# Input projection of a hybrid attention and Fourier layer: products of 2304 tokens, or seven block products in three passes

## The reference

```python
h = _rmsnorm(x, norm_g) * (1 + scale) + shift      # scale, shift, gate from silu(cond) @ w_ada + b_ada
z = h @ w_in                                       # 1024 -> 6176 channels
q, k, v, gate_a, r_f, r_b, u, gate_b, mg_a, mg_b = jnp.split(z, idx, axis=-1)
q, k = rope(q), rope(k); q = q * HEAD_DK ** -0.5
g_f = log_sigmoid(r_f @ w_af + b_af) / 16          # g_b likewise, from r_b
o = gla_scan(q, k, v, g_f) + reversed gla_scan(..., g_b)
y_a = (_rmsnorm(o) * silu(gate_a)) @ w_proj_a
y_b = (real(fft2(u)) @ w_four * silu(gate_b)) @ w_proj_b
x = x + gate * ((sigmoid(mg_a) * y_a + sigmoid(mg_b) * y_b) @ w_out)
```

## Time and profile before

| | |
|---|---|
| Runs | 2262.85, 2268.07, 2270.06 us; median 2268.07 |
| Profiled execution, from the first to the last instruction (span) | 2259.7 us |
| The shown median beside this span | 8.4 us above it |
| Instructions | 33049, of these 12121 matmuls |
| PE, PEld, DVE, ACT, POOL busy | 94%, 82%, 32%, 27%, 20% |
| DMA | 340.70 MB, 151 GB/s on average |

### The profile page before, as it was taken

The page is one execution under the profiler, slowest core; times in us unless marked ns, Lnnn a source line. Parts: engine busy times, 40 slices in busy tenths (PEclk is TensorE's granted clock), DMA queues, the critical chain, the costliest instruction groups (busy, mean ns, idle before and its releaser), DMA issues.

```text
span 2259.7 us, 33049 instructions
## 1 busy us (share of the span) xinstructions
PE 2129.4 (94%) x12121; PEld 1845.1 (82%) x12121; DVE 721.1 (32%) x1255; ACT 613.5 (27%) x1384; POOL 451.4 (20%) x340
## 2 busy tenths in 40 slices
PE   7699999999999999999999989998957999998998
PEld 2488889999888888888888867776857999997886
DVE  2867771000010001001001005557687222223423
ACT  2646661111111111111111116766523011012221
POOL 1500000000433223142322310004242111111212
PEclk9899999999999999999999989999978999999999
DMA  7334442212545445454544557554133343454443
GB/s 299 115 109 155 152 158 75 83 61 83 176 150 186 150 159 174 159 173 154 182 153 155 170 171 312 215 205 165 47 149 124 113 125 116 121 189 153 132 147 112
DMA packets 178437, 340.70 MB, mean 151 GB/s; under 512 B 14610, under 2 KB 120268, under 8 KB 173360
## 3 DMA queue, kind: packets, MB, share of 16 engines
q1 hardware_dynamic: 178352, 339.64, 43.2%
HBM read 215.84 MB, written 123.74 MB: 150 GB/s over the span
## 4 chain that ended last, share of the span: by engine, by line
PE 79%; issue 7%; DVE 6%; DMA 3%; ACT 3%; POOL 1%; SPq 0%; POOLq 0%; ACTq 0%; DVEq 0%
PE bank L1409 44%; PE bank L1613 15%; PE bank L1470 9%; PE bank L1498 3%; PE bank L1517 1%; PE bank L1519 1%; PE bank L1518 1%; PE bank L1505 1%; DMA x_in<-in_x 1%; ACT junk L770 1%; DVE zb L384 1%; POOL yt L750 1%; DVE uf L1267 1%; DVE h L1023 1%; PE bank L1526 1%
## 5 line engine op out<-in xcount | busy, mean ns | idle before, releaser
L1409 PE MATMUL bank<-h_hi,w_hi 128*128 128x512 f32 (+1 forms) x1640 | 606.3, 370 | 6.7 <-POOL h_lo L691 5.6
L1409 PE MATMUL bank<-h_lo,w_hi 128*128 128x512 f32 (+1 forms) x1640 | 605.4, 369 | 0.0
L1409 PE MATMUL bank<-h_hi,w_lo 128*128 128x512 f32 (+1 forms) x1640 | 604.4, 369 | 0.0
L1409 PEld LDWEIGHTS bank<-h_hi,w_hi 128*128 128x128 f32 x1640 | 310.2, 189 | 59.6 <-issue 5.8
L1409 PEld LDWEIGHTS bank<-h_hi,w_lo 128*128 128x128 f32 x1640 | 309.9, 189 | 52.5
L1409 PEld LDWEIGHTS bank<-h_lo,w_hi 128*128 128x128 f32 x1640 | 310.3, 189 | 51.5
L1057 DVE CAST w_hi<-w_raw 128x1024 fp32r<-128x1024 f32 x48 | 36.6, 762 | 870.2 <-PE bank L1409 672.8
L845 ACT ACTIVATE stage<-bank 128x512 f32<-128x512 f32 (+1 forms) x160 | 88.7, 555 | 682.0 <-PE bank L1409 682.0
L1613 PE MATMUL bank<-in_hi,pw_hi 128*128 128x256 f32 x864 | 245.9, 285 | 12.2 <-DVE in_lo L1292 12.2
L1613 PE MATMUL bank<-in_lo,pw_hi 128*128 128x256 f32 x864 | 245.6, 284 | 0.0
L1613 PE MATMUL bank<-in_hi,pw_lo 128*128 128x256 f32 x864 | 245.6, 284 | 0.0
(11 more groups left out here) (178 smaller groups left out, 2876.1 us busy)
## 6 DMA issues: line engine op xcount, KB each, us to landing
w_raw<-in_w_in SPq DMA_DIRECT2D x49, 512.0 KB, 3.9
dec_in<-e_dram SPq DMA_DIRECT2D x48, 384.0 KB, 3.5
rope<-in_rope SPq DMA_DIRECT2D x48, 384.0 KB, 4.1
qk_dec<-dec_in SPq DMA_DIRECT2D x48, 384.0 KB, 2.9
mg_ld<-mg_dram SPq DMA_DIRECT2D x72, 256.0 KB, 2.9
e_dram<-decs SPq DMA_DIRECT2D x32, 512.0 KB, 3.0
mg_dram<-stage SPq DMA_DIRECT2D x64, 256.0 KB, 2.0
wada<-in_w_ada SPq DMA_DIRECT2D x6, 2048.0 KB, 8.1
```

The costliest lines, as they stand in the source:

```text
L1409: ins = pe.matmul(bank[out][:, 0:n], w[0][:, k, sl], h[:, k, t0:t0 + n], start=(k == 0 and w is w_hi and h is h_hi), stop=(k == KT - 1 and ...
```

## The change

The input projection is written anew; the rank unit, the decays and the rotations are part of it.

- Tokens are taken in 3 passes of 768. In a pass, h is cut into four blocks: two halves of the inner dimension (A11 and A12, A21 and A22: 512 each) by two blocks of 384 tokens. The weights of a pair of units (2 x 128 channels) are cut the same way. Seven products of such blocks or of sums of them, 12 matmuls of 384 columns each (`product`), give the four quarters of the result, instead of eight. One pair of units is a window; a pass has 24 (`PAIRS`).
- POOL makes the sums of h once a pass (`sum_inputs`, `last_sum`) and the sums of weights for each window (`sum_weights`, 4 of 512 elements). ACT makes the high part of each of the seven weight operands of the next window (`high_weights`), DVE the low part (`low_weights`).
- The quarters are put together from PSUM in two banks and three tiles: ACT copies product 0 (`copy_first`) and moves out the first quarter (`first_quarter`), DVE makes five sums (`add_product`). Product 2 waits for the copy, product 3 for the first sum, 5 for the second and 6 for the third.
- Eight windows of a pass (`GATE_WINDOWS`) also make the gates of a head: two logit matmuls, two rounds of Relu, Abs, Exp, Ln on ACT, scans and a difference on DVE (`gate_sums`), two Exps on ACT (`decays`).
- q and k stay on chip: SP swaps their halves by a DMA within SBUF, POOL rotates (`rotate`, 3 instructions of 768 elements) and multiplies by the decays (`decay`, 1536 elements), and only qk_dec is stored. q_dram and e_dram go.
- v is made with channels in partitions and turned by PE transposes in the next window. The x tiles of the next pass are normalised, turned and modulated in windows 13 to 18, and split in window 23. Two adaLN rows move to the last pass.

The diff, cut to its core:

```diff
-RB = 384
+NP = 3
+BW = 384
+PW = 2 * BW
+TP = PW // P
+HK = KT // 2
+PAIRS = ([("qk", 0), ("u", 0), ("v", 0), ("qk", 1), ("u", 1), ("v", 1), ("qk", 2), ("v", 2), ("qk", 3), ("v", 3)]
+         + [("ga", i) for i in range(4)] + [("gb", i) for i in range(2)] + [("mg", i) for i in range(8)])
+NW = len(PAIRS)
+NPROD = 7
+RING = 8
+GATE_WINDOWS = (1, 2, 4, 5, 7, 8, 10, 11)
+X_WINDOWS = tuple(range(13, 13 + TP))
+ADA_WINDOWS = (15, 16)
+LOW_POOL_H = (4, 6)
...
-            def unit_block(slot, b, a, out):
-                t0, n = BLOCKS[b]
-                sl = slice(P * slot, P * slot + P)
-                for k in range(KT):
-                    for w, h in ((w_hi, h_hi), (w_hi, h_lo), (w_lo, h_hi)):
-                        ins = pe.matmul(bank[out][:, 0:n], w[0][:, k, sl], h[:, k, t0:t0 + n],
-                                        start=(k == 0 and w is w_hi and h is h_hi), stop=(k == KT - 1 and w is w_lo))
-                ins.then_inc(s_mm, 1)
...
+            def product(p, w, j):
+                n = NW * p + w
+                m = NPROD * n + j
+                slot = m % RING
+                bnk = bank[3 * (n % 2) + (0, 1, 0, 1, 2, 1, 2)[j]]
+                pe.wait_ge(s_wlo, m + 1)
+                if w == 0:
+                    input_split(p, j)
+                if j == 0 and n >= 2:
+                    pe.wait_ge(s_c11, n - 1)
+                elif j == 1 and n >= 2:
+                    pe.wait_ge(s_d, 5 * (n - 2) + 4)
+                elif j == 2:
+                    pe.wait_ge(s_p1, n + 1)
+                elif j == 3:
+                    pe.wait_ge(s_d, 5 * n + 1)
+                elif j == 4 and n >= 2:
+                    pe.wait_ge(s_d, 5 * (n - 2) + 5)
+                elif j == 5:
+                    pe.wait_ge(s_d, 5 * n + 2)
+                elif j == 6:
+                    pe.wait_ge(s_d, 5 * n + 3)
+                first = j in (0, 1, 4)
+                for k in range(HK):
+                    for wt, h in ((w_hi, h_hi), (w_hi, h_lo), (w_lo, h_hi)):
+                        ins = pe.matmul(bnk[:, 0:BW], wt[slot][:, k, :], h[:, j, k, :],
+                                        start=(first and k == 0 and wt is w_hi and h is h_hi),
+                                        stop=(k == HK - 1 and wt is w_lo),
+                                        skip_group_check=not first)
+                ins.then_inc(s_p, 1)
...
+            for p in range(NP):
+                for w in range(NW):
+                    uses = window_uses(p, w)
+                    for j in range(NPROD):
+                        product(p, w, j)
+                        for u in uses[j]:
+                            use(p, w, u)
...
+            def low_weights(n, j):
+                if n > LAST:
+                    return
+                m = NPROD * n + j
+                dve.wait_ge(s_whi, m + 1)
+                dve.tensor_tensor(w_lo[m % RING][:, :, :], w_op(n, j), w_hi[m % RING][:, :, :].bitcast(F32), ALU.subtract
+                                  ).then_inc(s_wlo, 1)
...
+            def add_product(n, step):
+                p, w, kind, i = pair(n)
+                b_bank, e_bank = bank[3 * (n % 2) + 1][:, 0:BW], bank[3 * (n % 2) + 2][:, 0:BW]
+                out, bnk, other, product = ((u2[:, :], b_bank, p1[:, :], 1), (u4[:, :], b_bank, p1[:, :], 3),
...
+                dve.wait_ge(s_p, NPROD * n + product + 1)
+                dve.tensor_tensor(out, bnk, other, ALU.add).then_inc(s_d, 1)
...
+            def gate_sums(p, i):
+                h, d, b = gate_unit(i)
+                g, at, t = 16 * p + i, 4 * d + h, TP * p + 3 * b
+                dve.wait_ge(s_ln, g + 1)
+                if g:
...
+                    if d:
+                        y, a, z = y[:, ::-1], a[:, ::-1], z[:, ::-1]
+                    ins = dve.tensor_tensor_scan(y, a, z, 0.0, ALU.add, ALU.add)
+                ins.then_inc(s_scan, 1)
+                dve.wait_ge(s_scan, g + 1)
...
+                dve.tensor_tensor(cc, cc, mid[:, at, t:t + 3].unsqueeze(2).to_broadcast([P, 3, P]), ALU.subtract
+                                  ).then_inc(s_bc, 1)
...
+            for p in range(NP):
+                for w in range(NW):
+                    n = NW * p + w
+                    final = p + 1 < NP and w + 1 == NW
+                    gates = [u[1] for j in range(NPROD) for u in window_uses(p, w)[j] if u[0] == "gate"]
+                    if n:
+                        add_product(n - 1, 4)
+                    low_weights(n + 1, 0)
...
+                    add_product(n, 0)
+                    low_weights(n + 1, 1)
...
+                        low_input(p + 1, 0)
+                    low_weights(n + 1, 2)
+                    if gates:
+                        gate_sums(p, gates[0])
+                    if final:
+                        low_input(p + 1, 1)
+                    add_product(n, 1)
+                    low_weights(n + 1, 3)
+                    if final:
+                        low_input(p + 1, 2)
+                    add_product(n, 2)
+                    low_weights(n + 1, 4)
+                    if gates:
+                        gate_sums(p, gates[1])
+                    if final:
+                        low_input(p + 1, 3)
+                    add_product(n, 3)
+                    low_weights(n + 1, 5)
+                    low_weights(n + 1, 6)
+                    if final:
...
+            def high_weights(n, j):
+                if n > LAST:
+                    return
+                m = NPROD * n + j
+                act.wait_ge(s_raw[n % 2], 16 * (n // 2 + 1))
+                if W_SUMS[j]:
+                    act.wait_ge(s_t, 4 * n + W_SUMS[j])
+                if m >= RING:
+                    act.wait_ge(s_p, m - RING + 1)
+                act.activation(w_hi[m % RING][:, :, :], w_op(n, j), ACT.Copy).then_inc(s_whi, 1)
...
+            def copy_first(n):
+                if n:
+                    act.wait_ge(s_d, 5 * (n - 1) + 4)
+                act.wait_ge(s_p, NPROD * n + 1)
+                act.activation(p1[:, :], bank[3 * (n % 2)][:, 0:BW], ACT.Copy).then_inc(s_p1, 1)
...
+            def gate_logs(p, w, i):
+                h, d, b = gate_unit(i)
+                g, k = 16 * p + i, use_number[p, w, ("gate", i)]
+                src, at = bank[6 + k % 2][:, 0:BW], 4 * d + h
+                if g:
+                    act.wait_ge(s_scan, g)
+                act.wait_ge(s_g, k + 1)
+                act.activation(relu[:, :], src, ACT.Relu, scale=-1.0, bias=nbal[:, at:at + 1])
+                act.activation(soft[:, :], src, ACT.Abs, bias=cols[:, C_BAF + at:C_BAF + at + 1]).then_inc(s_gc, 1)
+                act.wait_ge(s_gc, k + 1)
+                act.activation(soft[:, :], soft[:, :], ACT.Exp, scale=-1.0).then_inc(s_exp, 1)
+                act.wait_ge(s_exp, g + 1)
+                act.activation(soft[:, :], soft[:, :], ACT.Ln, bias=1.0).then_inc(s_ln, 1)
...
+            def decays(p, i):
+                h, d, b = gate_unit(i)
+                g = 16 * p + i
+                if i % 4 == 0 and g:
+                    act.wait_ge(s_qst, 32 * (4 * p + h))
+                act.wait_ge(s_bc, g + 1)
+                for sign in range(2):
+                    ins = act.activation(decs[:, sign, d, b * BW:b * BW + BW], cum[:, :], ACT.Exp,
...
+                        other_quarters(n - 1)
+                    high_weights(n + 1, 0)
+                    for i in waiting:
+                        decays(p, i)
+                    waiting = []
+                    if w in GATE_WINDOWS:
+                        act.preload_act_table_set("natural_log_exp_and_others")
...
+                    for j in range(NPROD):
+                        if j == 0:
+                            copy_first(n)
+                        elif j == 2:
+                            first_quarter(n)
+                        if j == 3:
+                            for i in waiting:
+                                decays(p, i)
+                            waiting = []
+                        for u in uses[j]:
+                            use(p, w, u)
+                            if u[0] == "gate":
+                                waiting.append(u[1])
+                        if j:
...
+            def sum_weights(n, which):
+                if n > LAST:
+                    return
+                raw, done = w_raw[n % 2], 4 * n
+                b11, b21 = raw[:, 0, 0:HK, :], raw[:, 0, HK:KT, :]
+                b12, b22 = raw[:, 1, 0:HK, :], raw[:, 1, HK:KT, :]
+                t1, t2, t4 = (w_sum[:, k, :, :] for k in range(3))
+                if which == 0:
+                    pool.wait_ge(s_raw[n % 2], 16 * (n // 2 + 1))
+                    if n:
+                        pool.wait_ge(s_wlo, NPROD * (n - 1) + 4)
+                    pool.tensor_tensor(t1, b12, b11, ALU.subtract).then_inc(s_t, 1)
+                    pool.wait_ge(s_t, done + 1)
+                    pool.tensor_tensor(b12, b12, b22, ALU.subtract).then_inc(s_t, 1)
```

(50 more changed lines are left out.)

1058 lines of the change are left out of this document (529 added, 529 removed).

## The result

| | before | seven products | ratio, 95% interval |
|---|---|---|---|
| Median | 2267.90 us | 2534.09 us | 1.1176 (1.116 to 1.1192) |
| Runs | 2262.85 to 2270.06 (4) | 2532.74 to 2536.47 (4) | |
| Span | 2259.7 us | 2532.6 us | |

The account below looks back on a forecast made before the run. TensorE, busy 94% of the span, was taken as the bound. Less matmul work and an earlier start gave -147.5 us net, stalls +265, sum +117.5: span 2377, median forecast 2386 us, slower; range 2200 to 2460 us.

Parts of the forecast that it names:

- Windows 1 to 12: Each pass's windows with gates, rotations and decays: 78 us of stalls a pass, 234 us in three passes.
- the walk: Window-by-window costing of windows 1 to 12 with collisions: 279 us against 183 of matmuls, 96 us of stalls a pass.
- The port's sum: DVE and POOL's SBUF port in windows 1 to 12: POOL 133 us plus DVE 58, 191 in 183 us of TensorE work.
- The low end: Windows 1 to 12 with an idle port: 24 us for gates, 11 tables, 11 late decay, 46 a pass.
- The price of 17.9 us for a gate window without contention: Gate windows, 8 a pass: waits before product 6 (counted from zero) add 3.0 us each, 72 us in 24 windows.
- The late decay: Windows 11 and 12: POOL waits for the last head's Exps, so window 13's weight sums come some 11 us late.
- Start: Before and in window 0: 768 tokens modulated by 58 us, window 0 ends at 90.5, rank unit at 97.5.
- Pass boundaries: Two boundaries between passes, where DVE and POOL make low parts beside the weights: 10 us each, 20 in all.
- Windows 13 to 23: Windows after the gates: squares and rotations of x delay product 2 by 0.9 us in 12 windows, 11 us.
- Rival 1: Projection: TensorE keeps its pace, stalls only 72 us, 2193 us, faster; decides while stalls stay under 147 us. Chance 0.22.
- Rival 3: Windows 1 to 12: the clock falls to 0.86 on average, adding 89 us, 2475 us. Chance 0.07.
- the prediction's chain: Gate windows: ACT and DVE steps through both gates take 9.4 us from product 2's end to product 6, counted from zero.

Follow-up runs that it names:

- s7: Seven-product kernel with POOL's rotations, decay products and weight sums all cut short (work left out), waits and gates kept: 2390 us.
- t1: Seven-product kernel, whole computation, with SP issuing the store of a v pair ahead of the next window's weights, swaps and decayed stores: 2497 us.
- s6: Seven-product kernel, whole computation, with the last head's decay products, their store, x loads and adaLN rows one window later: 2519 us.
- s5: Seven-product kernel, whole computation, with rank and gate weights copied and split inside the first window, no longer ahead of it: 2525 us.
- v1: Seven-product kernel with the first-window, late-decay, v-store, early-scan and ACT-order repairs, and POOL's rotations, decays and weight sums left short: 2265 us.
- s4: Seven-product kernel with 16 transposes of a constant added before products 4 and 6 (counted from one) of windows 1 to 12: 2533 us.
- u1: Seven-product kernel with 24 transposes of a constant added before product 6 (counted from one) of windows 1 to 12: 2544 us.
- v2: Reordered seven-product kernel (2399.28 us), whole computation, with POOL's rotations and decay products in pieces of 384 columns: 2363.93 us, ratio 1.043 to before.

## Why the prediction was wrong

**The size, step by step** (forecast span 2377, measured 2532.6):

- *Price of a matmul* 173.5 ns: the median spacing is 173. Right. The page of the Trainium skill "TensorE: Matmul & The Clock Gate" (Part 1) has columns / 2.4 GHz + 2.5 ns, 162.5: the measurement decides for the rows.
- *Windows 1 to 12*, the largest term: 78 us a pass forecast, (862 - 550) / 3 = 104 measured, 78 us more in three passes. The mechanism (handshakes and the port) was right and its size was not; the failed step is "I take 78, nearer the walk": the walk itself said 96, and 54 of those 78 us are that discount, for which no row spoke. Two things under it were short as well. The port's sum, "191 in 183 us", has its 58 us from the 84 splits alone (84 x 0.69); the scans and differences of 16 gates are some 25 more by the same rows, so it is 216. And the sum had the clock at nothing: 491 slow matmuls in these windows are 72 us, 24 a pass. How the missing 26 a pass divide between port, order and clock stays open. The low end, an idle port at 46 a pass, was measured: s7 has 60 a pass. So POOL's work is worth 44 a pass where I had 50 between the two ends. The price of 17.9 us for a gate window without contention holds in windows 2, 5 and 8 of s7 (17.3 to 18.7); 4 and 7, which wait for v's store, take 25 to 27, and 1, 10 and 11 20 to 25.
- *The walk was right in its sum only*, by errors that cancel: it gave windows 10 to 12 91 us (measured 82), windows 2, 5 and 8 73 (measured 60) and windows 1, 4, 7 and 9 75 (measured 104). What I had not seen are v's store, last on SP's queue (t1, -37 us), and in window 1 TensorE's wait of 2.84 us for DVE's rank parts. The late decay, 11 us a pass in the forecast, is worth 5 (s6).
- *Start*: "window 0 ends at 90.5 and the rank unit at 97.5" became 132.4, 35 us later. 14 of these stand ahead of all products: "768 tokens are modulated by 58" became 72.2. POOL makes the inverse roots of the norm behind four weight sums, TensorE waits 17.02 us for the normalised x, and three adaLN rows (48 records) stand behind that:

```profile
32.26 1.35 POOL L738 TENSOR_TENSOR rs<-rs,minus_half 128x6 f32<-128x6 f32 x1
```
```profile
37.76 2.82 PE L1591 MATMUL bank<-consts,x_a 128*128 128x128 f32 x12 [17.02 <-DVE x_d L1192]
...
41.80 21.17 PE L1581 MATMUL bank<-wada,silc 128*2 128x512 f32 x48
```

  I had also left out that ACT prepares the rank and gate weights ahead of the copy, with a DMA between (s5 gives 9 us back). POOL's two low parts took 8.3 us where 7 were forecast, and its sums 3.4 to 4.9 each for 3.5. That the first product started at 77.4, near the "as if from 76" of the forecast, is chance: 76 was the rank unit's end less its matmuls.
- *Pass boundaries*: 10 us each forecast, 13.5 measured. *Windows 13 to 23*: 11 us of stalls forecast, 42 measured. Squares, a weight copy and the sigmoid stand ahead of the copy: windows 14 to 18 last 17.3 us, 1.8 more than their 14.57 and 0.94 of transposes and not 0.9; window 19, where POOL sums three pieces of 1536 elements, takes 21.4 and was not costed; and each adaLN row took 7.1 us, not 3.5: one of these matmuls is two records of 0.43 us in the trace, and I had multiplied the code's 16 matmuls by the spacing of records.
- *Later stages*: +9 and not +3 us; why was not tried. *From span to median*: 1.5 us, not 8.4, which took 7 us off.

**Rivals.** Rival 1 named the right bound: v1, with 45 + 86 + 15 = 146 us of stalls by the table, is at break-even, and I had said that 147 decide. Rival 3 had the size of the clock's fall nearly right (89 us forecast, 85 measured as slow matmuls, at a chance of 0.07); its time, 2475, is also the forecast nearest to the 2534 measured. How much of the time it is stays open, since s4 and u1 took half of the slow matmuls away with transposes that cost about as much.

**Signs.** Spacing, gate windows over 18, idle time released by L1233 and the splits' mean were as forecast. The idle time stands before product 6 (the prediction's 5) with 126 us, behind the first gate, and before product 7 (its 6), behind the second gate, with 47; the prediction's chain ran through both gates to product 7. Windows 13 to 22 "near 15 to 16 us" failed for 14 to 19 of the first two passes. "Windows 10 to 12 the longest" held only just, ACT's waits for POOL's weight sums there were 2 us in the second pass, and my test that idle time at pass boundaries would prove me wrong was met in part.

**Open.** The 134 to 151 us were measured with POOL's work left out, not moved, and hold three things that were not parted: the port, POOL's lateness, and 17 to 30 us of slow matmuls that went with it (578 to 372, 467 to 312, 341 to 226). v2, which changes only the length of POOL's instructions, shows the port's waits by themselves: 35 us came back. Whether ACT could take the rotations or weight sums was not tried, nor a second set of gate buffers.

## What to carry to other kernels

Fewer matmuls turn a kernel bound by TensorE into one bound by handshakes: count for each product what must arrive within its 2 us, and on whose queue it stands behind what. Sum the port time of all of DVE's two-input SBUF operations and of POOL as one resource; if it exceeds the window, take the walk's number without a discount, and cut POOL's instructions short. What TensorE needs soon goes first on POOL too. A copy that TensorE waits for goes ahead of everything on ACT, and a buffer's store ahead of loads on SP.

## What was not expected of the hardware

- The length of an operation doesn't protect it: three 16-column scans took 0.35 us alone and 3.11 us beside POOL, and a copy of 128x3 elements 0.16 and 1.26 us.
- The same POOL work in shorter instructions made DVE faster although POOL was busy longer: 35 us less with 144 more instructions of POOL (I had written 288 before the run).
- After pauses of under 3 us the clock fell to half: in window 1 of the second pass TensorE stood still for 2.84 us up to 642.57 and for 2.78 us up to 655.88, and the granted clock was 0.50 (1.2 GHz) from 644 to 646 us and from 658 to 663. The spacing of a 384-column matmul was 320 ns there and 173 ns elsewhere. Keeping the clock up with transposes brought no gain: in u1 they delayed product 6 by 51 us in all where the faster matmuls gave back 44.
